# One of ten input projections made inside the last head of the first attention

## What is computed

```python
h = rmsnorm(x, ln1[l])
z = jnp.einsum('btd,de->bte', h, w_in[l])
u_pool, gq, gk, gv, gg, ga, fq, fk, fv, ff = jnp.split(z, pts, axis=-1)
y_pool = pool_mixer(u_pool, w_pool[l], pool_scale[l])
y_gla = gla_mixer(gq, gk, gv, gg, ga, w_a_up[l], b_a[l], gla_gn[l])
y_fox = fox_mixer(fq, fk, fv, ff, b_f[l])       # attention, 8 heads of 64
mix = jnp.concatenate([y_pool, y_gla, y_fox], axis=-1)
x = x + jnp.einsum('btd,de->bte', mix, w_o[l])
```

## Time and profile before

| | |
|---|---|
| median of 3 runs | 2082.71 us (2080.81 to 2083.56) |
| profiled execution, its own time | 2083.38 us |
| its span, first to last instruction | 2081.5 us |
| PE busy | 1980.6 us, 95% |
| POOL, DVE, ACT busy | 1102.0, 1145.6, 786.9 us |
| mean granted TensorE clock | 0.978 |

### The profile page before, as it was taken

How to read it: one execution, slowest core, us unless ns; L and a number is a source line. 1 busy time by engine, 2 the same in 40 slices (tenths; PEclk the granted TensorE clock), 3 DMA queues, 4 the chain that set the end, 5 groups by cost and what they waited for, 6 DMA issues and landing times.

```text
span 2081.5 us, 26580 instructions
## 1 busy us (share of the span) xinstructions
PE 1980.6 (95%) x9304; PEld 1597.9 (77%) x9304; DVE 1145.6 (55%) x1416; ACT 786.9 (38%) x1315; POOL 1102.0 (53%) x779
## 2 busy tenths in 40 slices
PE   4999999999999999999999999997999999989997
PEld 3767776887887888888888787885877778768785
DVE  6645443826376443444443485425788888863446
ACT  3335554223153222212213342012666666660422
POOL 1545555622735666665666764434555555653453
PEclk9999999999999999999999999998999999999998
DMA  4100000113211211111121132111001000001123
GB/s 145 47 27 11 21 21 21 41 41 112 91 51 41 61 55 47 49 53 60 42 60 52 60 107 66 41 52 41 11 21 30 20 20 20 20 31 51 41 73 119
DMA packets 30526, 102.69 MB, mean 49 GB/s; under 512 B 3330, under 2 KB 3522, under 8 KB 30452
## 3 DMA queue, kind: packets, MB, share of 16 engines
q1 hardware_dynamic: 26368, 91.94, 14.1%
q10 hardware_dynamic: 4084, 9.74, 1.3%
HBM read 97.31 MB, written 4.26 MB: 49 GB/s over the span
## 4 chain that ended last, share of the span: by engine, by line
PE 83%; DVE 7%; ACT 4%; issue 4%; POOL 1%; ACTq 0%; DMA 0%; DVEq 0%; POOLq 0%
PE ps L232 28%; PE ps L1537 18%; PE ps L385 9%; PE ps L1554 8%; PE ps L655 2%; PE ps L249 2%; PE ps L262 2%; PE ps L643 2%; PE ps L656 2%; PE ps L662 2%; DVE mx L756 1%; PE ps L642 1%; PE ps L641 1%; PE ps L685 1%; PE ps L687 1%
## 5 line engine op out<-in xcount | busy, mean ns | idle before, releaser
L2490 POOL TENSOR_TENSOR w_hi<-w_raw,zero 128x1024 fp32r<-128x1024 f32 (+2 forms) x107 | 197.3, 1844 | 408.7 <-PE ps L232 231.7
L711 POOL TENSOR_TENSOR probs_lo<-probs,mla_p_hi 128x512 fp32r<-128x512 f32 x192 | 191.2, 1015 | 168.6 <-ACT probs L704 166.7
L2492 POOL TENSOR_TENSOR w_lo<-w_raw,w_hi 128x1024 fp32r<-128x1024 f32 (+2 forms) x107 | 248.3, 2320 | 8.4
L1901 POOL TENSOR_TENSOR w_lo<-w_raw,w_hi 128x512 fp32r<-128x512 f32 x100 | 129.2, 1295 | 161.8 <-ACT w_hi L1659 161.2
L756 DVE TENSOR_REDUCE mx<-ps 128x1 f32<-128x128 f32 (+1 forms) x192 | 141.0, 754 | 79.5 <-PE ps L687 44.3
L232 PE MATMUL ps<-h_hi,w_lo 128*128 128x512 f32 x640 | 164.8, 400 | 0.2
L232 PE MATMUL ps<-h_hi,w_hi 128*128 128x512 f32 x640 | 158.1, 389 | 0.0
L711 POOL TENSOR_TENSOR probs_lo<-probs,fox_p_hi 128x512 fp32r<-128x512 f32 (+1 forms) x96 | 95.2, 1009 | 108.5 <-ACT probs L704 108.5
L1659 ACT ACTIVATE w_hi<-w_raw 128x512 fp32r<-128x512 f32 x100 | 62.2, 629 | 230.0 <-PE ps L1554 147.6
L232 PEld LDWEIGHTS ps<-h_hi,w_lo 128*128 128x128 f32 x640 | 120.7, 191 | 27.1 <-issue 2.7
L704 ACT ACTIVATE probs<-ps 128x512 f32<-128x512 f32 (+3 forms) x288 | 141.2, 490 | 0.0
(11 more groups left out here) (422 smaller groups left out, 4740.9 us busy)
## 6 DMA issues: line engine op xcount, KB each, us to landing
w_raw<-in_wpack SPq DMA_DIRECT2D x165, 512.0 KB, 3.5
x<-in_xT ACTq DMA_DIRECT2D x16, 512.0 KB, 7.5
out<-result SPq DMA_DIRECT2D x8, 512.0 KB, 2.9
p_raw<-in_pT ACTq DMA_DIRECT2D x1, 1024.0 KB, 5.0
pos_i<-in_pos SPq DMA_DIRECT2D x1, 512.0 KB, 6.4
const_stage<-in_consts SPq DMA_DIRECT2D x1, 404.0 KB, 3.2
vec<-in_vecs SPq DMA_DIRECT2D x1, 284.0 KB, 5.3
mla_q_hi<-c_neg ACTq DMA_DIRECT2D x16, 4.0 KB
```

The source lines that it names most:

```text
L711: nc.gpsimd.tensor_tensor(P_lo[g % 4][:, w], Pt[g % 4][:, w], A.p_hi[g % 2][:, w].bitcast(F32), ALU.subtract)\
L1901: nc.gpsimd.tensor_tensor(w_part(w_lo, p, b, odd, j), src, w_part(w_hi, p, b, odd, j).bitcast(F32), ALU.subtract).then_inc(done, 1)
L2490: nc.gpsimd.tensor_tensor(w_hi[s][:, kts, :], raw[s][:, kts, :], no_change[:, kts, :], ALU.add).then_inc(w_hi_done, 1)
L2492: nc.gpsimd.tensor_tensor(w_lo[s][:, kts, :], raw[s][:, kts, :], w_hi[s][:, kts, :].bitcast(F32), ALU.subtract)\
```

## The change

`last_pe` gets the number of a unit. Where it is given (the first attention, unit 13), the first half of that unit's projection, 24 matmuls, is made ahead of the last head's scores, and the second half's 24 are dealt out two behind each piece. `rest_pe` starts with i = 1, the gate matmuls stand behind projection 1, and ACT's `store(0)` moves ahead of its wait for `g_gate`. The second attention calls `last_pe` without a unit and is unchanged.

```diff
-        def last_pe(pe, A):
+        def last_pe(pe, A, unit=None):
+            if unit is not None:
+                pe.wait_ge(w_split, unit + 3)
+                project(pe, unit % 2, range(DT), h_hi, h_lo, pjA, done=False, halves=(0,))
             pe.wait_ge(A.row_in[1], 16 * (A.heads // 2))
             for g in range(2):
                 score_pe(pe, A, A.heads - 1, 1, g)
-            attend_pe(pe, A, A.heads - 1, 1)
+            steps = [(w, a, kt) for w, a in ((w_lo, h_hi), (w_hi, h_lo), (w_hi, h_hi)) for kt in range(DT)]
+            each = len(steps) // N_PIECES
+            def part(g):
+                for n in range(each * g, len(steps) if g == N_PIECES - 1 else each * (g + 1)):
+                    w, a, kt = steps[n]
+                    last = nc.tensor.matmul(pjA[:, 1, :], w[unit % 2][:, kt, :], a[:, kt, cols(1)], start=(n == 0), stop=(n == len(steps) - 1))
+                if g == N_PIECES - 1:
+                    last.then_inc(unit_done, 1)
+            attend_pe(pe, A, A.heads - 1, 1, part if unit is not None else ())
...
         def rest_pe(pe):
-            for i in range(N_REST):
+            for i in range(1, N_REST):
...
-                if i == 0:
+                if i == 1:
                     pe.wait_ge(small_read, 1)
                     pe.wait_ge(fox.norm_done, 2 * FOX_H)
...
         def rest_act(act):
+            def store(i, fn=ACT.Copy):
...
+            store(0)
             act.wait_ge(g_gate, 1)
...
-            def store(i, fn=ACT.Copy):
...
-            store(0)
             store(1)
...
-            last_pe(pe, fox)
+            last_pe(pe, fox, U_REST)
```

More of the change, by code:

```diff
@@ L1234, in rest_act @@
         def rest_act(act):
+            def store(i, fn=ACT.Copy):
+                act.wait_ge(unit_done, U_REST + i + 3)
+                dst = z8[:, i, :] if i < 8 else zg[:, i - 8, :]
+                nc.scalar.activation(dst, flat((pjA, pjB)[i % 2]), fn).then_inc(rest_read, 1)
+            store(0)
             act.wait_ge(g_gate, 1)
@@ L1243, in rest_act @@
             nc.scalar.activation(tau(g1), tau(g1), ACT.Ln, bias=one).then_inc(g_act, 1)
-            def store(i, fn=ACT.Copy):
-                act.wait_ge(unit_done, U_REST + i + 3)
-                dst = z8[:, i, :] if i < 8 else zg[:, i - 8, :]
-                nc.scalar.activation(dst, flat((pjA, pjB)[i % 2]), fn).then_inc(rest_read, 1)
-            store(0)
             store(1)
```

## The result

The changed kernel takes 2085.42 us (median of 20 executions, 2080.18 to 2088.81), the kernel before 2080.84 us (20, 2077.66 to 2083.56). The ratio of the two is **1.0018, 95% interval 1.0012 to 1.0023**: 3.8 us more (2.5 to 4.8); the two medians lie 4.6 us apart. A second comparison, made with the experiments, gave 1.0006 (0.9996 to 1.0016), 1.2 us more. The first comparison shows a small loss about as large as that limit, the second none that is clear of its noise.

A forecast was written before the change was run, and what follows sets the result against it. PE was taken to bound the kernel. At projection 4, 391.3 + 1.7 - 390.66 was summed to +2.4 us on the profiled 2083.38: 2085.8, or 2085.1 by the median; range 2080.5 to 2089.0.

The forecast's parts named there:

- that limit: Whole kernel: the smallest difference a measurement can tell from no change, 0.2% or 4.2 us.
- The two costs and the one gain: Gain: 7.2 us by projection 0's end; costs: 3.3 us idle ahead of projection 1, 2.9 to 4.6 ahead of projection 4.
- the bound of 342.9 for head 7: End of head 7 and projection 0 if switching between kinds of matmul costs nothing; forecast 345.4.
- The fill: Head 7: moved matmuls fill PE's idle; head and projection 0 end at 345.4 instead of 352.65, 7.2 us won.
- The split without its cover: Ahead of projection 1: POOL's unit 14 split no longer hidden, PE idles 3.3 us, projection 1 starts at 348.7.
- The chain behind the gate: Gate's end to store(2) stays 26.4 us; projection 4 waits 2.9 to 4.6 us and starts at 391.3.
- The first rival: Ahead of projection 4: store(2) doesn't hold PE, start at 388.4, time 2080.5; chance 0.10.
- The clock: Behind each new wait, ahead of projections 1 and 4: low clock costs 1.7 us, bounds 0 and 3.1.
- the collision: Behind projection 2: POOL's unit 17 split runs ahead of DVE's scan, store(2) 2.7 us later, time 2087.8; chance 0.22.

The follow-up runs named there:

- Experiment 4: Changed kernel with the second half's 24 matmuls in one block behind head 7's last values, not among the pieces; ratio to the kernel before 0.9996.
- experiment 10: Changed kernel with early unit 14 split, early store(2), and the second half in one block behind head 7's last values; ratio to the kernel before 0.9980.
- 3: Changed kernel with both POOL's unit 14 split ahead of head 7's subtractions and store(2) ahead of the g_dve wait; ratio to the kernel before 0.9963.
- Experiment 1: Changed kernel with POOL's split of unit 14 moved ahead of head 7's twelve subtractions; ratio to the kernel before 0.9978.
- Experiment 8: Changed kernel with the gate matmuls moved back ahead of projection 1; ratio to the kernel before 0.9993.
- experiment 2: Changed kernel with ACT's store(2) moved ahead of its wait for g_dve 5; ratio to the kernel before 0.9978.
- experiment 5: The changed kernel run again, unaltered, for a second trace; ratio to the kernel before 1.0006.

## Why the prediction was right

The two costs and the one gain are there, in their places and near their sizes. Two things were luck. The median, 2085.42 us, lies 0.3 us from the forecast 2085.1, but the kernel before measured 2080.84 this time and not 2082.71, so the difference was not the forecast one. And the difference itself, 2.4, lies between two patterns of which the forecast describes neither. Two slips in the sums change nothing: 391.3 + 1.7 - 390.66 is 2.34, and the bound of 342.9 for head 7 leaves out the 0.8 us of waits as well as the switching.

*The fill.* Forecast 345.4 for the end of head 7, with projection 0; measured 344.98 in a trace whose L694 is 0.1 us later than before. Two successive values at 338.58 and 340.22 stand 1.64 us apart, where I had counted about 1.7, and without a mask two stand 1.63 us apart (335.19 and 336.82), 0.04 more than seven matmuls of 0.227, where I had put 0.1 for the switching. The wait for the first exponential was 0.29 us, and none for a subtraction; I had put 0.8 for the two. Experiment 4 shows the idle and the first half alone; experiment 10 against 3 shows the second half alone.

*The split without its cover.* Forecast 3.3 us of idle and projection 1 at 348.7; measured 3.09 and 348.07. Experiment 1 removes this wait and leaves the second. Either of the two waits taken away alone gives 0.9978, so both together make this change worth nothing.

*The chain behind the gate.* Forecast 26.4 us to projection 4, and a wait of 2.9 to 4.6; measured 26.5 and 2.87 in one trace, 28.7 and 6.61 in the other. Experiment 8 gives back the third projection and the wait is gone, experiment 2 takes the store out of the chain and it is gone too. The first rival (store(2) doesn't hold PE) falls.

*The clock.* This is the term that I put together wrongly, though the sum came out near. I charged 1.7 us for low clock behind each of the two waits and said that the clock behind the gate would not matter. The sizes were right: 12.72 against 11.10 us behind the first wait, 12.68 against 10.88 behind the second. But in the first trace no low clock followed the first wait, so 1.7 of my 2.4 fall away, and as projection 1 also started a little earlier than forecast, +0.3 is left. In the second trace it did, and the clock stayed full behind the gate, which set off the collision and made +4.2. The low stretches and the collision are not independent cases with chances of their own. In the changed kernel's two traces they come as two patterns: low behind the gate and a split during the scan, or low behind the first wait and a split ahead of the scan. What the clock does in each, the traces of the other kernels bear out, three of three and nine of nine (experiment 5). My forecast of +2.4 is neither, and lies between. The chance of 0.22 for the collision was low: sixteen of twenty executions and six of twelve lie in the upper group, and the one trace from that group shows it. That all of those executions have this collision is inferred from their times and that one trace. Which pattern an execution takes no run here decides.

*The collision.* Its point of decision was given as 11.3 us behind the gate; the projection that set it off ended at 11.2. Its size was put at 2.7 us and was 2.2.

The Trainium skill's rule (SBUF — State Buffer, section Who interferes with whom), that the instruction issued first takes the shared ports and the other one waits for all of it, has its case in the 0.1 us between 374.10 and 374.20. For the split behind head 7 the same section lets DVE's instructions with one input in SBUF pass beside POOL, and the trace agrees: of the changed kernel's split behind head 7 the second half ran beside DVE's three norms and took 2.34 us, and the next split's second half, with DVE idle, took 2.39.

## What to carry to other kernels

Work that is moved into a gap may have covered something where it stood. Ask what ran beside it, and how much of the gap's gain that takes back: here a split of 4.3 us had hidden under the moved projection, and moving the split as well, into a stretch where its engine stood idle, is an edit of three lines that turned +0.1 to +0.2% into -0.2%. Where an event in the middle of a series moves by one place, count the distance from it to each consumer in the series on both sides. And where an engine's queue holds a short, ready instruction behind a long wait, put it ahead: here store(2) could have run when projection 2 was done, at 375.4 us, 7 us before the wait for `g_dve` ended, and it held up the bottleneck from the place behind it.

## What was not expected of the hardware

Whether POOL's split began 0.1 us ahead of DVE's scan or 1.5 us behind its start made 2.2 of the 3.7 us by which a wait of PE grew from 2.87 to 6.61; the other 1.5 came from the full clock ahead of it. Holding POOL back until L1329 was done saved DVE 1.5 us and won next to nothing, since the next pair of instructions collided instead (a split took 8.3 us that takes 4.3 alone). Idles of 3.09 us, equal in length, were followed by a low clock in one trace and not in the other. And the gate matmuls (16 rows deep, 3.6 to 4.1 us without a gap) brought a low clock in nine traces of nine where the projection ahead of them had run at full clock, and in none of three where a low stretch had come at its start.
